# A two-layer decoder trunk in fp32: another order for attention's first projections, an earlier split of their third weight chunk, and another order in the first norm

## The reference, cut to what matters

```python
for layer in range(2):                       # x: (1, 1024, 1024) float32
    xn = rms_norm(x, g[0])
    if layer == 0:
        mix = short_conv(xn, conv_in_w, conv_w, conv_out_w)   # 3 gates, taps of width 3
    else:
        k, v = split(rms_norm(x, kv_norm_g) @ kv_w)           # shared K and V
        q = (xn @ q_w) * HEAD_DIM ** -0.5                     # 16 heads of 64
        mix = dilated_window_attention(q, k, v) @ o_w         # 3 dilations, ALiBi, merged
    x = x + rms_norm(mix, g[1])
    x = x + rms_norm(swiglu(rms_norm(x, g[2]), ffn_in_w, ffn_out_w), g[3])
```

## Time and profile before

| | us |
|---|---|
| median of 3 runs | 2330.35 (2328.69 to 2331.31) |
| the profiled execution | 2329.61 |
| its span | 2327.8 |
| PE busy in the span | 2252.7 (97%) |
| DVE, ACT, POOL busy | 1511.4, 940.5, 477.8 |

### The profile page before, as it was taken

One profiled execution on the slowest core, in us unless ns is written; L12 is line 12 of the kernel. 1 busy time (PEld: TensorE's weight loads), 2 busy tenths in 40 slices (PEclk: granted clock), 3 DMA queues, 4 the chain that ended last, 5 costly groups with the idle time before them and its releaser, 6 DMA issues.

```text
span 2327.8 us, 32020 instructions
## 1 busy us (share of the span) xinstructions
PE 2252.7 (97%) x10792; PEld 1886.3 (81%) x10792; DVE 1511.4 (65%) x2236; ACT 940.5 (40%) x1712; POOL 477.8 (21%) x415
## 2 busy tenths in 40 slices
PE   7999997999999999999999999999799999999998
PEld 6888786888888888877888888888688888888886
DVE  5333347766666667797666666575876666666768
ACT  4111135322323234464655656564532223323443
POOL 1000014433233101153000000001543333220103
PEclk9999998999999999999999999999899999999999
DMA  4111122333333377735323323243233333337764
GB/s 145 46 54 45 54 91 67 94 105 109 106 108 103 112 259 250 242 104 172 80 67 73 82 69 72 69 114 112 65 95 101 109 104 108 108 110 255 250 232 167
DMA packets 244852, 273.96 MB, mean 118 GB/s; under 512 B 18400, under 2 KB 157664, under 8 KB 242656
## 3 DMA queue, kind: packets, MB, share of 16 engines
q1 hardware_dynamic: 241504, 260.64, 37.1%
q10 hardware_dynamic: 3200, 11.54, 1.4%
HBM read 198.20 MB, written 48.76 MB: 106 GB/s over the span
## 4 chain that ended last, share of the span: by engine, by line
PE 89%; DVE 4%; issue 3%; POOL 2%; ACT 1%; DMA 1%; SPq 0%; DVEq 0%; POOLq 0%; ACTq 0%
PE banks L1086 35%; PE banks L1133 15%; PE banks L880 11%; PE banks L1178 9%; PE banks L1009 7%; PE banks L1215 3%; PE banks L1244 3%; PE banks L1230 3%; PE banks L928 1%; PE banks L1258 1%; POOL xb_low L2724 1%; PE banks L1330 1%; DVE down_split L2205 1%; DMA raw_second<-in_o_w 1%; POOL sums L2798 0%
## 5 line engine op out<-in xcount | busy, mean ns | idle before, releaser
L1086 PE MATMUL banks<-xb_mid,up_split 128*128 128x512 f32 x2112 | 497.4, 391 | 4.2 <-DVE t_tile L1974 4.2
L1086 PEld LDWEIGHTS banks<-xb_mid,up_split 128*128 128x128 f32 x2112 | 398.7, 189 | 87.9 <-issue 5.0
L1133 PE MATMUL banks<-down_split 128*128 128x512 f32 x1848 | 422.3, 390 | 3.3 <-DVE down_split L2205 2.4
L1133 PEld LDWEIGHTS banks<-down_split 128*128 128x128 f32 x1848 | 345.8, 188 | 78.0 <-DVE down_split L2205 6.5
L1086 PE MATMUL banks<-xb_low,up_split 128*128 128x512 f32 x1584 | 373.6, 389 | 2.7 <-DVE third_gate L2286 2.7
L1086 PEld LDWEIGHTS banks<-xb_low,up_split 128*128 128x128 f32 x1584 | 297.2, 188 | 65.1 <-issue 3.5
L2205 DVE TENSOR_TENSOR down_split<-down_raw,down_split 128x1024 fp32r<-128x1024 f32 x154 | 197.9, 1285 | 102.3 <-ACT down_split L1637 102.0
L1637 ACT CAST down_split<-down_raw 128x1024 fp32r<-128x1024 f32 x154 | 162.1, 1053 | 211.5 <-PE banks L1133 174.3
L2048 DVE TENSOR_TENSOR up_split<-sums,up_split 128x512 fp32r<-128x512 f32 x176 | 157.7, 897 | 130.1 <-ACT up_split L1492 129.8
L880 PE MATMUL banks<-x_hi,w_first 128*128 128x512 f32 x768 | 184.4, 392 | 1.2 <-ACT x_hi L1411 1.1
L2798 POOL TENSOR_TENSOR sums<-raw_up 128x512 f32<-128x512 f32 x88 | 119.7, 1361 | 320.2 <-DVE up_split L2048 162.5
(11 more groups left out here) (180 smaller groups left out, 3315.0 us busy)
## 6 DMA issues: line engine op xcount, KB each, us to landing
raw_up<-in_ffn_in_w SPq DMA_DIRECT2D x88, 512.0 KB, 5.2
down_raw<-in_ffn_out_w SPq DMA_DIRECT2D x154, 256.0 KB, 3.4
down_raw<-hid_spill SPq DMA_DIRECT2D x154, 256.0 KB, 4.0
hid_spill<-hid_mix SPq DMA_DIRECT2D x110, 256.0 KB, 2.2
down_second<-in_ffn_out_w SPq DMA_DIRECT2D x66, 256.0 KB, 3.1
k_stack<-k_parts SPq DMA_DIRECT2D x32, 512.0 KB, 6.2
raw_first<-in_conv_in_w SPq DMA_DIRECT2D x24, 512.0 KB, 3.7
hid_spill<-hid SPq DMA_DIRECT2D x44, 256.0 KB, 2.4
```

What stands on the lines that cost most here:

```text
L1086: mm = pe.matmul(bank(b_out), up_split[:, p, a, q * P:(q + 1) * P], block(RIGHT_OF[p], b)[:, q, :], start=(i == 0), stop=(i == len(passes) ...
L1133: mm = pe.matmul(bank(b_out), side[:, a, 0, i * P:(i + 1) * P], side[:, b, 1, :], start=(p in (M3, M5, M1, M2) and first and j == 0), stop ...
```

## The change

The six half products come in the order K0, V0, Q0, K1, V1, Q1 (digits are token halves) where it was K0, V0, K1, Q0, V1, Q1. Tile 7 is turned ahead of matmul 56, inside Q0, where it was ahead of matmul 48, the first of K1. The wait for norm2's last low part moves with K1. The third chunk (Q's weights) is scaled, cast and subtracted inside `down_layer`: POOL's `scale_chunk(2)` comes ahead of the four `gain_left`, ACT's cast ahead of norm2's high parts of tiles 5 and 6, DVE's subtraction ahead of their low parts. ACT's and DVE's lists behind it follow the new order. In the first norm the calls are written out: the high part of tile 2, the first weight chunk and the high part of tile 3 come ahead of the square of tile 4 on ACT; on DVE tile 3 is normed ahead of the low part of tile 1, and the first weight chunk is subtracted ahead of the low part of tile 3. SP's list is the same.

```diff
-        OPENING = ((0, 0), (1, 0), (0, 1), (2, 0), (1, 1), (2, 1))
-        TURNS = {22: HT, 36: HT + 1, 46: HT + 2, 48: HT + 3}
+        OPENING = ((0, 0), (1, 0), (2, 0), (0, 1), (1, 1), (2, 1))
+        TURNS = {22: HT, 36: HT + 1, 46: HT + 2, 56: HT + 3}
...
                     if pos == 2:
-                        pe.wait_ge(*xl_ready.at("norm2", TT))
                         pe.wait_ge(*k_lo_done.at("attn", 1))
                     elif pos == 3:
+                        pe.wait_ge(*xl_ready.at("norm2", TT))
                         pe.wait_ge(*v_done.at("attn", 1))
...
@@ ACT, norm0
-                for i in range(TT + lag_split):
...
+                for t in range(3):
+                    second_square("norm0", t)
+                high_part("norm0", 0)
+                second_square("norm0", 3)
+                high_part("norm0", 1)
+                high_part("norm0", 2)
+                prepare(0)
+                high_part("norm0", 3)
+                second_square("norm0", 4)
+                prepare(1)
...
@@ ACT and DVE, down_layer, behind the loop over the rounds
+                    prepare(chunk0["attn"] + 2)
                     for t in range(HT + 1, TT - 1):
...
@@ POOL, down_layer, between the loop over the rounds and gain_left
+                if pre:
+                    scale_chunk(2)
                 for i in range(HT):
                     gain_left(i)
...
@@ DVE, ahead of attention
             project((0, 0), 0, OPENING)
             low_part("norm2", TT - 1)
-            prepare(chunk0["attn"] + 2)
             distances()
             window_counts(0)
+            project((0, 0), 2, OPENING)
             window_counts(1)
-            project((0, 0), 2, OPENING)
+            values_low((0, 0), 0, TURN)
+            project((0, 0), 3, OPENING)
             prepare(chunk0["attn"] + 3)
```

More of the change, by code:

```diff
@@ L1319, in project_first @@
                     if pos == 2:
-                        pe.wait_ge(*xl_ready.at("norm2", TT))
                         pe.wait_ge(*k_lo_done.at("attn", 1))
                     elif pos == 3:
+                        pe.wait_ge(*xl_ready.at("norm2", TT))
                         pe.wait_ge(*v_done.at("attn", 1))
                     elif pos == 4:
+                        pe.wait_ge(*q_lo_done.at("attn", 1))
+                    elif pos == 5:
                         pe.wait_ge(*k_lo_done.at("attn", 2))
-                    elif pos == 5:
-                        pe.wait_ge(*q_lo_done.at("attn", 1))
                 n, k = i // KT, i % KT
@@ L1494, in norm0 @@
             def norm0():
-                _, _, _, lag_split = LAG["norm0"]
-                for i in range(TT + lag_split):
-                    if i in (TT // 2, TT // 2 + 2):
-                        prepare((i - TT // 2) // 2)
-                    if i < TT:
-                        second_square("norm0", i)
-                    if i >= lag_split:
-                        high_part("norm0", i - lag_split)
+                for t in range(3):
[8 more added lines that the diff above has]
+                prepare(1)
+                second_square("norm0", 5)
+                high_part("norm0", 4)
+                second_square("norm0", 6)
+                high_part("norm0", 5)
+                second_square("norm0", 7)
+                high_part("norm0", 6)
+                high_part("norm0", 7)
             def output_square(ph, t):
@@ L1871, in _ @@
             project((0, 0), 0, OPENING)
+            project((0, 0), 1, OPENING)
             high_part("norm2", TT - 1)
-            prepare(chunk0["attn"] + 2)
-            project((0, 0), 1, OPENING)
             project((0, 0), 2, OPENING)
-            prepare(chunk0["attn"] + 3)
             values_high((0, 0), 0, TURN)
             project((0, 0), 3, OPENING)
+            prepare(chunk0["attn"] + 3)
             project((0, 0), 4, OPENING)
@@ L2051, in norm0 @@
             def norm0():
-                _, _, lag_xn, lag_split = LAG["norm0"]
                 dve.wait_ge(pre_in, 16 * pres["norm0"])
-                for i in range(TT + lag_split):
-                    if i == TT // 2 + 2:
-                        prepare(0)
-                        prepare(1)
-                    if i >= lag_split:
-                        low_part("norm0", i - lag_split)
-                    if 0 <= i - lag_xn < TT:
-                        normed("norm0", i - lag_xn)
+                normed("norm0", 0)
+                normed("norm0", 1)
+                low_part("norm0", 0)
+                normed("norm0", 2)
+                normed("norm0", 3)
+                low_part("norm0", 1)
+                low_part("norm0", 2)
+                prepare(0)
+                low_part("norm0", 3)
+                normed("norm0", 4)
+                prepare(1)
+                normed("norm0", 5)
+                low_part("norm0", 4)
+                normed("norm0", 6)
+                low_part("norm0", 5)
+                normed("norm0", 7)
+                low_part("norm0", 6)
+                low_part("norm0", 7)
             def mixer_norm(ph, norm_ph):
@@ L2588, in _ @@
             low_part("norm2", TT - 1)
-            prepare(chunk0["attn"] + 2)
             distances()
             window_counts(0)
+            project((0, 0), 2, OPENING)
             window_counts(1)
-            project((0, 0), 2, OPENING)
+            values_low((0, 0), 0, TURN)
+            project((0, 0), 3, OPENING)
             prepare(chunk0["attn"] + 3)
-            values_low((0, 0), 0, TURN)
             window_counts(2)
-            project((0, 0), 3, OPENING)
             masked_logs()
@@ L2846, in scale_pair @@
                     scale_chunk(3 * (fixed + 1) + c, moving if isinstance(moving, int) else moving * 3)
-            for c in (2, 3, 4):
+            for c in (3, 4):
                 scale_chunk(c)
```

## The result

The changed kernel takes 2341.24 us in the median of 5 runs (2338.02 to 2343.88), beside 2331.31 (2328.69 to 2332.99) for the kernel before: a ratio of 1.0041, 95% interval 1.0030 to 1.0052, or +9.9 us by the medians. Measured a second time, beside other kernels, it came out at 2339.58 against 2330.99, 1.0037 (1.0023 to 1.0051), +8.6. It is slower by about 0.4%. The profiled execution took 2339.12 us, its span 2336.3, which is 8.5 more than before.

The account below looks back on a forecast made before the run. PE, busy 97%, was taken as the bound, with the chain K1, copies, first score almost level. +8.0 + 1.0 - 0.2 = +8.8 on the profiled 2329.61 gave 2338.4, 2339.0 as median; range 2333 to 2342.5.

Parts of the forecast that it names:

- POOL's rest of 13 us doesn't help: POOL ahead of norm2: gain_left queued behind the third chunk's load and scaling delays tile 4's normed by 2.4 us.
- The wait changes its name: PE before Q0: the 2.4 us wait for norm2's last low part isn't covered; Q0 waits for K0's low part instead.
- Both branches of the start of Q0: Q0 starts at 1064.5 and runs cold, or at 1066.1, likely warm, if tile 4's 3.4 us gap costs a cold start.
- K's last low part, +8.0: End of K1 in the half products: K's last low part at 1079.4 against 1071.42, +8.0 us.
- The copies move whole: DMA chain behind K's last low part: its 16.95 us shifts unshortened, first softmax step at 1098.6, +8.0.
- The rival in which they run faster once alone: Copies behind K1 run at 373 GB/s, done by 1090; change costs +2.1 and half a microsecond, 2333; chance 0.06.
- DVE's table, "ahead of the DMAs, decides nothing": DVE before the first softmax step: its table of biases ends near 1092 to 1094, ahead of the copies.
- Cold at attention's start, +1.0: Attention's first matmuls run cold after the wait for q_stack: up to 1.9 us, taken as 1.0.
- From there PE has work throughout, and nothing gives time back: After attention's start PE always has work, so none of the loss is recovered.
- The first norm, -0.2: Opening of the kernel: PE's first products wait slightly less with the new call order, -0.2 us, bounds -1.15 and +0.6.

Follow-up runs that it names:

- both repairs: Changed kernel with POOL's third scaling behind the four gain_left and K's copies split by token half, against the kernel before: 2334.92 us, 1.0016, +3.9.

## Why the prediction was right, point by point

- **The result.** Forecast 2339.0 in 2333.0 to 2342.5, slower; measured 2341.24, and 2339.58 the second time. In the profile the sum was +8.8 on the execution, which took +9.5. That the sum is this close is in part luck: the parts were off by up to 0.8 us in both directions, and a cold start elsewhere, named below, had its share.
- **POOL's rest of 13 us doesn't help.** Right in its cause: `gain_left` was queued behind a load that landed at about 1036. Sized at +2.4, measured +3.0 (1052.35 against 1049.33). The row behind the difference is the load: it took 4.6 us and not 3.9, and so the last split met the scaling for longer (2.87 us in place of about 2.5), and the last rounds started 0.57 us later, where I had them even. In the second execution the load took 4.1 and the same start was 0.16 late. Taking the scaling behind `gain_left` took the 3.4 us of waiting away (0.97).
- **The wait changes its name.** Right: 2.6 for K0's low part in place of 2.4 for norm2's. Both branches of the start of Q0 came true, one in each profile: 1066.20 with the cold start ahead of it (forecast 1066.1), 1064.68 without (forecast 1064.5).
- **K's last low part, +8.0.** Measured 1080.04, +8.6, with the cold ten matmuls (4.11 against 2.56) in it, and 1081.07 in the other execution.
- **The copies move whole.** Right: 16.7 us (17.4 in the second execution) against 16.95, and the first softmax step at 1098.07, 0.5 us under the 1098.6 forecast (1099.73 in the second). The rival in which they run faster once alone fell with the profile: from 1080.1 to 1096.7 the DMA engines moved 190 GB/s and were 84% busy. Why these copies move 190 to 212 GB/s where the stretch ahead of them moved 373, no run here shows. That they were the chain is shown by splitting them, which took the wait away (6.0 and 7.6 us in the two profiles of the changed kernel, none in the run with split copies).
- **DVE's table, "ahead of the DMAs, decides nothing".** True of the changed kernel: it ended at 1093.38, and DVE stood idle for 4.08 us behind it. But I held it for slack, and it was a second bound: with the copies out of the way it ended at 1096.1, because most of it is listed behind K's last low part. A price for "the copies" alone promised 4 us (the expectation of that run), and the medians gave 2.
- **Cold at attention's start, +1.0.** Too little in the profiled execution: the softmax's fourth step was +9.3 where the first was +7.5, so 1.8 us. In the second it was 1.1 (+10.3 and +9.2), so the size isn't fixed.
- **From there PE has work throughout, and nothing gives time back.** Not so in the profiles. At 1470 the changed kernel is 9.4 us behind, at 1555 only 7.5. Between the two, at the end of attention, PE has a gap of 2.85 us in the kernel before and then runs at a clock of 0.57 for 4 us; in the changed kernel it has 2.57 us and stays at 1.00. The second execution shows the same (10.2 us behind, then 8.0). All six profiles without the whole change were cold at this place, and three of the eight with it (the repaired kernels included), so that chance has a part in these 2 us; how large a part, these runs can't tell. Some 1.0 us (1.3 in the second) are lost again by the end of the span, and where stays open.
- **The first norm, -0.2.** PE's first product came at 19.64 in place of 19.84, just as forecast. The ratio of this part alone was 0.9995 (0.9986 to 1.0004): nothing to be told from zero.
- **The sum of what was found.** New order alone +8.3, early chunk alone +4.8, order with the chunk behind `gain_left` +5.9, all of it +8.6 to +9.9; three repairs (gains first, copies by half, table ahead of K) bring it to +0.6 (0.9993 to 1.0011). The loss is how late K's second half is, passed on by two lists that begin at it, SP's copies and DVE's table; with both lists repaired the order is level. No run shows it better. The kernel before with split copies came out at -2.3, which would put the new order some 3 us (0.6 + 2.3) behind it even then; but each of the two comparisons has about 2 us on either side, and in the two profiles the first softmax steps stand 0.3 us apart (1089.44 and 1089.14), so that this isn't shown.

## What to carry to other kernels

Before a product is put off to hide a wait, list what is queued behind it on every engine and on the DMA queue, not only the longest chain: here a chain of copies (16.7 us) hid a chain of DVE steps (13.3 us in the changed kernel, 15.2 to 15.5 in the runs where it was the bound) that began at the same event. Repairing the copies alone gave 2 us by the medians and moved the wait to the other chain; the DVE chain by itself was not repaired in any run. Work that is to shorten such a chain must cross the event at its head; moved from one gap to another ahead of it, it changed nothing here. And a step put ahead of a queue because its engine rests must have its input there already, or the rest becomes everybody's wait.

## What the runs showed of the hardware

**A cold start behind the same gap comes and goes.** The runs hold the same piece of program with equal gaps ahead of it. Behind 2.36 us K1's first eight matmuls ran at half clock in part in two executions (the kernel before, and with the first norm's order) and warm in two (both with K's copies split and the old order). Behind 3.10 to 3.12 us Q0 ran cold in five executions and warm in one, the run with the table moved across K's last low part. Behind 3.38 to 3.43 us the ten matmuls after tile 4's turn took 4.1 to 4.4 us three times and 2.55 twice; where they were warm, the next gap of 3.1 us was followed by a cold start, and where they were cold with the new order, the next gap of 2.6 us was not (twice). With the early chunk alone both were, 3.38 and then 2.77 us, and so was the one start behind 3.49 us, with the new order alone. The rows below show the same eight matmuls behind the same gap, in the run with both repairs and the table's first steps moved, and in the one with the table moved across K's last low part; the granted clocks from 1064 to 1068 were 0.57 and 1.00.

```profile
1063.82 3.23 PE L1340 MATMUL banks<-x_hi,w_second 128*128 128x512 f32 x8 [3.11 <-DVE k_parts L2485]
```

```profile
1063.72 2.09 PE L1340 MATMUL banks<-x_hi,w_second 128*128 128x512 f32 x8 [3.11 <-DVE k_parts L2485]
```

It is worth 1.6 us at the end of that product (8.26 us from its first matmul to ACT's part, against 6.67), which may be a good part of the scatter between executions of one kernel (2338.02 to 2343.88 for the changed one). The Trainium skill's page "TensorE: Matmul & The Clock Gate" (section "What's actually happening") says that the number of cold matmuls varies from run to run of one kernel. The two executions of the changed kernel agree: behind the same 3.42 us the ten matmuls took 4.11 and 2.55. So one profile can't say whether a gap of 2.4 to 3.4 us costs a cold start; the gaps of 4.2 us and more at attention's start did each time (eight profiles, clocks of 0.50 to 0.68 from 1096 to 1100).

**DVE and POOL.** From 1018 to 1112, in all fourteen profiles, a step of DVE that started while a POOL scaling or gain ran, and that was 128x512 or larger with all its inputs in SBUF, ended a fixed time behind it: 1.07 to 1.08 us for one with two inputs of 128x1024, and 0.55 for one with a single input or with two of 128x512. The FFN's split took 2.87 and 2.35 us in the two profiles of the changed kernel (1.23 alone), two steps of the table 2.80 each (1.22 alone), and with the two repairs a step of 0.69 took 2.38. Steps with an input in PSUM were not held up: norm2's low part at 1059.58 in the kernel before took 1.23 us inside two scalings. Where such a DVE step had started first, POOL's scaling took longer instead, up to 2.97 us in place of 1.90. For the DVE step a meeting cost 0.2 to 1.7 us, and which step it hits changes with every microsecond of shift.
